# A hybrid decoder's mixer: where the roots of the means are taken, and who evicts keys, values and probabilities

## What is computed

```python
def mixer_projections(x, norm_g, w_in, q_norm_g, k_norm_g):
    h = rmsnorm(x, norm_g)
    q, k, v, ua, ub = jnp.split(h @ w_in, [512, 640, 768, 1280], axis=-1)
    q = rmsnorm(q.reshape(*lead, 8, 64), q_norm_g)
    k = rmsnorm(k.reshape(*lead, 2, 64), k_norm_g)
    return q, k, v.reshape(*lead, 2, 64), ua * jax.nn.sigmoid(ub)

attn = swa_prompt(q, k, v, sinks)       # window 128, ALiBi, a sink per head
conv = conv_module(u, past, ...)        # depthwise, 31 taps; LayerNorm; silu
x = x + concat(attn, conv) @ w_out
x = x + cross_attend(x, mem_k, mem_v, ...)
x = x + hier_moe(rmsnorm(x, norm_ffn_g), ...)   # top 2 of 8 experts in one of 4 groups
```

## Time and profile before

| | us |
|---|---|
| median of 3 runs | 1477.09 |
| lowest and highest | 1475.53 and 1477.17 |
| the profiled execution | 1473.9 |
| its span | 1472.1 |
| TensorE busy | 1273.6 (87%) |
| VectorE busy | 775.6 (53%) |
| ScalarE busy | 283.2 (19%) |
| GpSimd busy | 150.3 (10%) |

### The profile page before, as it was taken

The page is one execution under the profiler, slowest core; times in us unless marked ns, Lnnn a source line. Parts: engine busy times, 40 slices in busy tenths (PEclk is TensorE's granted clock), DMA queues, the critical chain, the costliest instruction groups (busy, mean ns, idle before and its releaser), DMA issues.

```text
span 1472.1 us, 17784 instructions
## 1 busy us (share of the span) xinstructions
PE 1273.6 (87%) x6455; PEld 651.0 (44%) x6455; DVE 775.6 (53%) x2215; ACT 283.2 (19%) x812; POOL 150.3 (10%) x205
## 2 busy tenths in 40 slices
PE   7979699999999947787999999998599998899970
PEld 3435445554554433353555565655333433333430
DVE  1116789999898994231344445544435224434416
ACT  1123224433433341030111111111001110110100
POOL 0000001001100000100000000000100022132104
PEclk9998799999999968798999999998599999999995
DMA  8695000300000030372115110002379999999916
GB/s 329 245 351 181 1 22 1 143 30 16 14 29 15 1 141 29 128 264 115 29 43 215 43 43 15 1 15 100 127 297 384 356 407 418 417 416 416 389 67 222
DMA packets 68320, 238.27 MB, mean 162 GB/s; under 512 B 14112, under 2 KB 28358, under 8 KB 54387
## 3 DMA queue, kind: packets, MB, share of 16 engines
q1 hardware_dynamic: 56235, 217.20, 38.5%
q0 software_dynamic: 11424, 17.85, 3.5%
q10 hardware_dynamic: 576, 2.10, 0.4%
HBM read 216.27 MB, written 45.77 MB: 178 GB/s over the span
## 4 chain that ended last, share of the span: by engine, by line
PE 71%; DVE 13%; DMA 6%; issue 5%; ACT 2%; POOL 1%; SPq 1%; DVEq 0%; ACTq 0%; POOLq 0%
PE bank L777 24%; PE bank L1194 11%; PE bank L1147 9%; PE bank L1201 7%; DVE W L1605 6%; PE bank L976 3%; DMA W<-in_w_exp_down 3%; PE bank L1125 2%; PE bank L1085 2%; PE bank L820 2%; PE bank L1181 2%; DVE G L1550 1%; PE bank L889 1%; PE bank L1161 1%; DMA W<-in_cache_mem_k 1%
## 5 line engine op out<-in xcount | busy, mean ns | idle before, releaser
L777 PE MATMUL bank<-W,G 128*128 128x512 f32 (+3 forms) x864 | 354.0, 566 | 4.2 <-DVE G L1550 3.4
L1605 DVE SCALAR_TENSOR_TENSOR W<-W,dwT 128x128 f32<-128x128 f32 (+1 forms) x1080 | 280.3, 337 | 0.0
L777 PEld LDWEIGHTS bank<-W,G 128*128 128x128 f32 (+1 forms) x864 | 158.6, 187 | 176.2 <-issue 170.0
L1194 PE MATMUL bank<-W 128*32 128x512 f32 (+1 forms) x1600 | 204.9, 612 | 15.9 <-issue 14.2
L976 PE MATMUL bank<-W 128*128 128x512 f32 (+1 forms) x288 | 129.9, 610 | 11.7 <-DVE W L1711 7.8
L1194 PEld LDWEIGHTS bank<-W 128*32 128x32 f32 (+1 forms) x1600 | 65.4, 116 | 150.8 <-issue 148.4
L1147 PE MATMUL bank<-W 128*128 128x512 f32 (+1 forms) x288 | 128.2, 599 | 0.8 <-DVE W L1875 0.6
L659 POOL TENSOR_SCALAR st<-st 128x1 f32<-128x1 f32 (+5 forms) x58 | 13.2, 228 | 948.9 <-DVE st L1681 276.4
L1201 PE MATMUL bank<-W 128*32 128x512 f32 (+1 forms) x800 | 105.9, 610 | 4.1 <-DMA W<-in_w_exp_down 3.0
L2046 DVE TENSOR_TENSOR W<-bank,cvec 128x512 f32<-128x512 f32 x56 | 36.3, 687 | 131.3 <-PE bank L1181 131.2
L976 PEld LDWEIGHTS bank<-W 128*128 128x128 f32 (+1 forms) x288 | 54.0, 190 | 81.8 <-issue 81.6
(11 more groups left out here) (287 smaller groups left out, 1350.6 us busy)
## 6 DMA issues: line engine op xcount, KB each, us to landing
W<-in_w_exp_gate SPq DMA_DIRECT2D x36, 1024.0 KB, 11.5
W<-in_w_exp_up SPq DMA_DIRECT2D x36, 1024.0 KB, 15.6
W<-in_w_exp_down SPq DMA_DIRECT2D x36, 1024.0 KB, 15.5
y_scratch<-W SPq DMA_DIRECT2D x28, 512.0 KB, 12.7
y_scratch<-LG SPq DMA_DIRECT2D x1, 11264.0 KB
W<-in_cache_mem_k SPq DMA_DIRECT2D x8, 1024.0 KB, 5.3
W<-in_cache_mem_v SPq DMA_DIRECT2D x8, 1024.0 KB, 7.8
W<-in_w_in SPq DMA_DIRECT2D x4, 1792.0 KB, 25.1
```

The costliest lines, as they stand in the source:

```text
L777: mm = pe.matmul(bank[0:rows, at:at + hi - lo], HT[:, c, 0:rows], w[:, c, lo:hi], start=(c == 0), stop=(c == DC - 1))
L1194: mm = pe.matmul(B[2 + par][lo:hi, :], HG[par][:, c, lo:hi], WGU[u][:, :, c, :], start=(c == 0), stop=(c == DC - 1), skip_group_check=True)
L1605: dve.scalar_tensor_tensor(y, src, w, y, ALU.mult, ALU.add).then_inc(M["conv_tap"], 1)
```

## The change

In the mixer, for the x of blocks 1 to 8 and for all queries and keys, ScalarE takes the square root of mean plus epsilon (`root`) and VectorE its reciprocal; GpSimd keeps the layer norm's root, those of the memory stage, of block 0's x and of the later stages. ScalarE takes over three evictions from VectorE: turned keys (`KT`), values (`VV`), and the last four heads' turned probabilities of the second key tile. TensorE turns keys ahead of queries, and waits for both halves of `take_hT` ahead of the scores. The squares use the tiles of queries and keys as scratch, no longer Z. The x sums, roots and norms of blocks 1 and 2 move to earlier places: block 1's sum and root ahead of the loop, its norm behind `take_hT` of turn 0; block 2's sum and root behind the exponentials of turn 1, its norm ahead of VectorE's probability copy of turn 1. In turn 0 the squares stand ahead of the gate. All taps of block 0 stand in one run ahead of that norm, and for the other blocks the cut at 80 becomes 84.

```diff
@@ TensorE
+                    pe.wait_ge(M["kn_ready"], s2 + 1)
+                    pe.wait_ge(M["v_ready"], s2 + 1)
+                    pe.transpose(B[3][:, 256:256 + n2], KN[0:n2, :], ident[0:n2, 0:n2]).then_inc(M["kT_done"], 1)
                     for j in range(4):
...
-                    pe.wait_ge(M["kn_ready"], s2 + 1)
-                    pe.wait_ge(M["v_ready"], s2 + 1)
-                    pe.transpose(B[3][:, 256:256 + n2], KN[0:n2, :], ident[0:n2, 0:n2]).then_inc(M["kT_done"], 1)
 
                     pe.wait_ge(M["qT_ready"], s2 + 1)
                     pe.wait_ge(M["kT_ready"], s2 + 1)
+                    if s1 < NT:
+                        pe.wait_ge(M["ht_ready"], 2 * (s1 + 3))
@@ ScalarE
+            def root(dst, src, count, done):
+                act.activation(dst, src, ACT.Sqrt, bias=eps_col[0:dst.shape[0], :], scale=1.0 / count).then_inc(M[done], 1)
+
+            def root_x(n, rows):
+                act.wait_ge(M["x_sq"], n + 1)
+                root(st[0:rows, 2 + n % 2:3 + n % 2], st[0:rows, n % 2:n % 2 + 1], D, "x_rt")
+
+            def squares(s1):
+
+                n1 = rows_of(s1)
+                act.wait_ge(M["pkv_done"], AFTER["pkv_done"] + s1 + 1)
...
+                act.activation(VV[s1 % 3][0:n1, :], B[3][0:n1, 128:256], ACT.Copy).then_inc(M["v_ready"], 1)
+                act.wait_ge(M["pq_done"], s1 + 1)
...
+            act.wait_ge(x_in[3], 16)
+            sum_sq(3, rows_of(1), XR[3])
+            root_x(3, rows_of(1))
+
             for it in range(NT + 2):
                 s1, s2, s3 = it, it - 1, it - 2
                 if 0 <= s2 < NT:
                     n2 = rows_of(s2)
+                    act.wait_ge(M["kT_done"], s2 + 1)
+                    if s2 >= 2:
+                        act.wait_ge(M["sc_done"], 4 * (s2 - 1))
+                    act.activation(KT[s2 % 3][:, 0:n2], B[3][:, 256:256 + n2], ACT.Copy).then_inc(M["kT_ready"], 1)
...
+                if s2 == 0:
+                    act.wait_ge(x_in[0], 32)
+                    sum_sq(4, rows_of(2), XR[0], view(W, RMO + 1024, D))
+                    root_x(4, rows_of(2))
...
+                if s1 == 0:
+                    squares(0)
...
+                    if len(kts) == 2:
+                        act.wait_ge(M["ptD_done"], seen + 2)
...
+                            act.activation(pt[:, 1, 4:8, :], B[6][:, :].rearrange("p (h t) -> p h t", h=4), ACT.Copy).then_inc(M["ptA_ready"], 1)
+                if 1 <= s1 < NT:
+                    squares(s1)
...
+                    if s1 >= 2 and nxt < NT:
...
+                        sum_sq(nxt + 2, rows_of(nxt), XR[(nxt + 2) % 4])
+                        root_x(nxt + 2, rows_of(nxt))
+                    act.wait_ge(M["qk_ssq"], AFTER["qk_ssq"] + 2 * s1 + 2)
+                    root(st[0:n1, 22:32], st[0:n1, 12:22], HD, "qk_rs")
@@ VectorE
-                dve.wait_ge(M["x_rs"], n + 1)
+                if 3 <= n < NT + 2:
+                    dve.wait_ge(M["x_rt"], n - 2)
+                    link(dve.reciprocal(st[0:rows, 2 + n % 2:3 + n % 2], st[0:rows, 2 + n % 2:3 + n % 2]))
...
-            CUTS = [28, 40, 60, 68, 80, 116]
+            CUTS = [28, 40, 60, 68, 84, 116]
...
+                    if s1 == 0:
+                        norm_z(3, rows_of(1), XR[3])
...
-                    dve.tensor_copy(KT[s2 % 3][:, 0:n2], B[3][:, 256:256 + n2]).then_inc(M["kT_ready"], 1)
...
-                    conv_taps(s2, CUTS[2], CUTS[3])
+                    conv_taps(s2, CUTS[2], CUTS[3] if s2 else CC * TAPS)
...
+                    if s2 == 0:
+                        norm_z(4, rows_of(2), XR[0])
...
-                    dve.tensor_copy(VV[s1 % 3][0:n1, :], B[3][0:n1, 128:256]).then_inc(M["v_ready"], 1)
...
                     dve.wait_ge(M["qk_rs"], AFTER["qk_rs"] + s1 + 1)
+                    link(dve.reciprocal(st[0:n1, 22:32], st[0:n1, 22:32]))
```

More of the change, by code:

```diff
@@ L1282, in _, with sum_sq @@
             act.activation(cvec[:, 0:8], B[6][:, 0:8], ACT.Copy).then_inc(M["vec_ready"], 1)
-            def sum_sq(n, rows, src):
-                act.activation(JUNK[0:rows, :], src[0:rows, :], ACT.Square, accum_out=st[0:rows, n % 2:n % 2 + 1]).then_inc(M["x_sq"], 1)
+            def sum_sq(n, rows, src, junk=JUNK):
+                act.activation(junk[0:rows, :], src[0:rows, :], ACT.Square, accum_out=st[0:rows, n % 2:n % 2 + 1]).then_inc(M["x_sq"], 1)
             act.wait_ge(x_in[0], 16)
@@ L1313, in _ @@
                 act.dma_start(o["mem_v"][0, 0, m * 128:(m + 1) * 128].rearrange("t h d -> t (h d)"), MV[:, m, :]).then_inc(M["mem_out"], 16)
+            def root(dst, src, count, done):
[6 more added lines that the diff above has]
+                act.wait_ge(M["pkv_done"], AFTER["pkv_done"] + s1 + 1)
+                if s1 >= 1:
+                    act.wait_ge(M["kT_done"], s1)
+                for h in range(KVH):
+                    a = act.activation(KN[0:n1, HD * h:HD * h + HD], B[3][0:n1, HD * h:HD * h + HD], ACT.Square, accum_out=st[0:n1, 20 + h:21 + h])
+                a.then_inc(M["qk_ssq"], 1)
+                if s1 >= 3:
+                    act.wait_ge(M["pvA_done"], s1 - 1)
+                    act.wait_ge(M["pvD_done"], s1 - 1)
+                act.activation(VV[s1 % 3][0:n1, :], B[3][0:n1, 128:256], ACT.Copy).then_inc(M["v_ready"], 1)
+                act.wait_ge(M["pq_done"], s1 + 1)
+                for h in range(HEADS):
+                    a = act.activation(QN[0:n1, HD * h:HD * h + HD], B[2][0:n1, HD * h:HD * h + HD], ACT.Square, accum_out=st[0:n1, 12 + h:13 + h])
+                a.then_inc(M["qk_ssq"], 1)
+            act.wait_ge(x_in[3], 16)
+            sum_sq(3, rows_of(1), XR[3])
+            root_x(3, rows_of(1))
             for it in range(NT + 2):
@@ L1550, in take_hT @@
                     dve.tensor_tensor(HT[:, 4 * half:4 * half + 4, 0:rows], src, gain(v + 4 * half, 4, rows), ALU.mult).then_inc(M["ht_ready"], 1)
+            link(dve.memset(eps_col, EPS))
             link(dve.memset(LG[:, :], 0.0))
@@ L1702, in _ @@
                 if 0 <= s2 < NT:
-                    for k, kt in enumerate(kts):
-                        nk = n2 if s2 == 0 and kt else 128
-                        dve.wait_ge(M["ptD_done"], seen + k + 1)
-                        if k == 0 and s2 >= 1:
-                            dve.wait_ge(M["pvD_done"], s2)
-                        if s2 == 0:
-                            dve.tensor_copy(pt[0:nk, kt, 1, :], B[6 if k else 1][0:nk, 0:256]).then_inc(M["ptD_ready"], 1)
-                        else:
-                            dve.tensor_copy(pt[:, kt, 4:8, :], B[6 if k else 1][:, :].rearrange("p (h t) -> p h t", h=4)).then_inc(M["ptD_ready"], 1)
+                    if s2 == 0:
+                        norm_z(4, rows_of(2), XR[0])
+                    dve.wait_ge(M["ptD_done"], seen + 1)
+                    if s2 >= 1:
+                        dve.wait_ge(M["pvD_done"], s2)
+                    if s2 == 0:
+                        dve.tensor_copy(pt[:, 0, 1, :], B[1][:, 0:256]).then_inc(M["ptD_ready"], 1)
+                    else:
+                        dve.tensor_copy(pt[:, kts[0], 4:8, :], B[1][:, :].rearrange("p (h t) -> p h t", h=4)).then_inc(M["ptD_ready"], 1)
                 if s1 < NT:
```

65 lines of the change are left out of this document (21 added, 44 removed).

## The result

The changed kernel takes 1450.96 us (median of 4 runs, 1449.94 to 1451.92), against 1477.13 for the kernel before in the same comparison: a ratio of 0.9816, 95% interval 0.9800 to 0.9832. The forecast was 1451.4.

The account below looks back on a forecast made before the run. A full turn was taken as bound by a loop through TensorE, ScalarE with GpSimd, and VectorE. First turns 14.0, full turns 6.2, tail 1.3 and clock 4.2 sum to 25.7: 1477.09 - 25.7 = 1451.4 us, range 1447.5 to 1461.

Parts of the forecast that it names:

- The bound: Full mixer turn: a loop of 30.3 us TensorE, 5.7 us ScalarE and GpSimd, 14.3 us VectorE.
- The full turn: Mixer, spans between scores of turns 2 to 8: -1.03 us a turn, -6.2 over six.
- cancel within 0.13 us: Full turn: x root done at 351.15 with ScalarE's new work, against 351.28 with GpSimd's two roots.
- The clock: TensorE's falls to 1.2 GHz at scores: none expected at a 1.2 us gap; -4.2, between 0 and -4.2.
- The first turns: Turns 0 and 1, new order of squares, roots and norms: scores of turn 2 at 148.1 against 162.15, -14.0 us.
- 2.8 us of slack: Turn 1, x rows of block 2: margin used in the slower rival (chance 0.03, 1489.6 us).
- The third rival: First turns gain only once, as gate or x rows come later or half clock lasts; 8.7 lost, 1460; chance 0.10.
- The tail: Turn 9, without projection, up to w_out: start gains 0.1, score eviction 1.2 us earlier; -1.3 in all.
- 1.2 us earlier: Turn 9: VectorE's first score eviction, earlier because its 8 taps are done while it waits.
- The sum: All terms together: 14.0 + 6.2 + 1.3 + 4.2 = 25.7 us gained.
- the further 0.12: Working on chances: beside 0.60 for the forecast, a rest of about 0.12 said to be left out.
- the rival's 1466.7: Table switches on ScalarE cost twice, 1.38 us more around each load; 10.4 us gained, 1466.7; chance 0.05.

Follow-up runs that it names:

- two_loads: The change plus a one-column exponential ahead of the x root of turns 2 to 7, forcing a second table load; 1469.71 us in one run.
- cuts80: The change with the cut back at 80 in place of 84, so twelve taps ahead of the norm; 1459.0 us, ratio 0.9858.
- evict_only: The kernel before with only the evictions moved to ScalarE; roots on GpSimd, old first turns, cut at 80; 1481.39 us, ratio 1.001.
- x_late: The change with the load of block 2's x issued behind the sample block's 24 stores; 1450.21 us, ratio 0.9799.
- fill_later: The change with the 11 MB zero fill and three cache moves issued behind block 2's x load and the sample block's stores; 1446.21 us, ratio 0.9769.
- roots_only: The kernel before with only ScalarE's roots and VectorE's two reciprocals; evictions, cuts and first turns as before; 1473.92 us, ratio 0.9954.

## Why the prediction was right, and where it was not

- **The bound** (a loop of TensorE, ScalarE and VectorE) was right: a root 1.50 us later costs 1.50 us a turn (two_loads), taps behind it cost 1.05 (cuts80), and work taken off VectorE without touching the root brings nothing (evict_only).
- **The full turn** was put at -1.03 and measured -0.90. The forecast itself has the cut as its one large term: roots and evictions "cancel within 0.13 us", and the 32 taps in place of 36 are the -1.06. cuts80 bears that out, with +0.15 for the first and -1.05 for the cut. Against the start of the scores of turn 5, the norm moved from 35.94 to 36.04 (+0.10; I had +0.07), and L1550 from 48.57 to 47.87 (-0.70; I had -0.79). Small parts make up the rest: the two reciprocals with their links cost 0.45 in place of 0.40, and the hand-over to the scores 0.15 in place of 0.1. Six spans brought 5.4 and not 6.2.
- **The clock** was put at -4.2. From the scores of turn 2 to those of turn 8 it was 306.72 us and is 297.10: 9.62 less, of which 6 x 0.90 = 5.4 are the turns and 4.2 the falls. This was the least certain of the large terms. The 0 of 48 above agrees with its reason, a narrower gap, without showing what makes a single turn fall.
- **The first turns** were put at -14.0 and measured -14.4 from the first projection (86.12 to 71.70), and -13.1 to -13.7 by the three other traces with this code, so the closeness of the 14.4 is in part luck. Each step on the way stood within a microsecond: the scores of turn 1 gained 5.0 (5.4 predicted), the gate waited for the stores until 138.12 (137.33), TensorE's second transposes began at 140.07 (139.2). The working has two slips. Its terms behind the gate add up to 146.75 and not 147.1. And it gives block 2's x 2.8 us of slack, counted up to the gate's sigmoid, though the first transposes of turn 1 need the scaled probabilities by the end of the projections, which by its own figures leaves 0.6; measured, the scaling ended at 137.07 and the first transposes began at 138.50, so 1.4. x_late shows it: 4.6 us later, and 3.2 of them already show there. The third rival, which lost 8.7 of it, didn't come. x_late shows that later x rows do cost; a gate later than here was not run, only an earlier one (fill_later).
- **The tail** was wrong in size: -1.3 predicted. Turn 9's start gained 0.27 and the way to its w_out 0.58, so 0.85. From there to the end of the last w_out it was 44.90 us and is 46.03, so 1.13 are lost again, with a mean granted clock of 0.81 in place of 0.85. So the tail as a whole, from the scores of turn 9 to the end of the last w_out, is 0.55 us longer. The steps that failed are the clock, which the tail's sum left out, and the eviction that I let start "1.2 us earlier". VectorE in the order of time, which answers to the earlier trace rows:

```profile
491.40 2.19 DVE L1645 SCALAR_TENSOR_TENSOR W<-W,dwT 128x128 f32<-128x128 f32 x8
494.89 2.74 DVE L1684 SCALAR_TENSOR_TENSOR W<-W,bank 128x256 f32<-128x256 f32 x8 [1.30 <-PE bank L889]
```

  The taps are done early, as said, but then VectorE waits 1.30 us for TensorE: the first pair of scores comes 1.27 us after their start, not 0.6, so only 0.6 of my 1.2 was there.
- **The sum** for the profiled execution was 25.7 and is 23.9: 14.4 + 9.6 + 0.3, less 0.55 in the tail and less 0.5 for a later start, and 0.6 from the rest. The medians differ by 26.2, since the profiled execution of before was 3.2 under its median and that of the change only 0.9. So the agreement of 1451.4 with 1450.96 is luck by about 2 us: the steps behind it are 1.8 short in sum, and the medians make it up. The chances of the forecast and its rivals add up to 1.00, so the further 0.12 that the working speaks of has no place in them.
- **The rule of the Trainium skill** ("ScalarE: Activation LUTs", "What ACT_TABLE_LOAD costs"), by which a switch costs 2.66 us, did not hold, and nor did the rival's 1466.7, an estimate that goes with it. The load is 1.28 us, and the next activation starts 1.29 us after its start in each of the rows above. Its advice to batch by set ("Table sets: the hidden batching unit") would have spoken against the roots on ScalarE. They pay one more load a turn and still gain 0.24 us of it (roots_only), since load and roots took the place of GpSimd's 1.96 and 0.55 us.
